# Hybrid decoder block on 8 cores: the constants on VectorE are prepared behind the third conv channel tile instead of ahead of the first scalings of x

## The reference

```python
h = concat([meta, x])                                # (B, 16 + 2048, 1024)
u = rms_norm(h, norm_mix_g) @ w_in                   # 2576 columns
c_val, c_gate, q, k, v, g, gate_lr = split(u)
# conv group, 512 channels
y = depthwise_causal_conv(c_val * sigmoid(c_gate), conv_w, width=31) + conv_b
y_conv = silu(layer_norm(y) * conv_ln_g + conv_ln_b)
# gated linear attention, 4 heads, chunks of 64
log_a = log_sigmoid(gate_lr @ w_gate2 + gate_b) / 16
y_gla = rms_norm(chunked_attention(q, k, v, log_a), gla_norm_g) * silu(g)
h = h + concat([y_conv, y_gla]) @ w_out
h = h + (silu(n @ w_ffn_gate) * (n @ w_ffn_up)) @ w_ffn_down     # n = rms_norm(h, norm_ffn_g)
return rms_norm(h, norm_final_g)[:, 16:]
```

## Time and profile before

| | |
|---|---|
| median of 3 runs | 1551.28 us |
| time of the profiled execution | 1555.21 us |
| its span on the slowest core (core 4) | 1553.7 us |
| spans of the 8 cores | 1530.8 to 1553.7 us |
| TensorE busy | 1444.6 us, 93% |
| VectorE, ScalarE, GpSimd busy | 790.7, 546.5, 266.8 us |
| DMA | 297.55 MB moved, mean 192 GB/s |
| mean granted TensorE clock, cores | 0.983 to 0.989 |

### The profile page before, as it was taken

How to read it: one execution, slowest core, us unless ns; L and a number is a source line. 1 busy time by engine, 2 the same in 40 slices (tenths; PEclk the granted TensorE clock), 3 DMA queues, 4 the chain that set the end, 5 groups by cost and what they waited for, 6 DMA issues and landing times.

```text
span 1553.7 us, 26365 instructions; the slowest of 8 cores (1530.8 to 1553.7 us)
## 1 busy us (share of the span) xinstructions
PE 1444.6 (93%) x8290; PEld 690.4 (44%) x8290; DVE 790.7 (51%) x1739; ACT 546.5 (35%) x964; POOL 266.8 (17%) x359
## 2 busy tenths in 40 slices
PE   0878799999999999999999999999999999999995
PEld 0444454444444444444444444444444445444442
DVE  2368448525565246544384445744475454744324
ACT  2465362415424254224433054222542245211101
POOL 2042151122510123001400024001320023000000
PEclk9989899999999999999999999999999999999998
DMA  9568898899978984499745986379744975365551
GB/s 185 130 165 206 189 199 172 180 233 270 252 203 208 253 272 129 137 201 250 231 136 159 215 247 197 126 199 249 232 141 144 219 243 181 123 197 175 198 163 55
DMA packets 127992, 297.55 MB, mean 192 GB/s; under 512 B 48992, under 2 KB 59616, under 8 KB 127856
## 3 DMA queue, kind: packets, MB, share of 16 engines
q1 hardware_dynamic: 65424, 199.92, 40.6%
q0 software_dynamic: 23904, 86.49, 25.3%
q10 hardware_dynamic: 38528, 9.44, 4.7%
HBM read 276.22 MB, written 46.40 MB: 208 GB/s over the span
## 4 chain that ended last, share of the span: by engine, by line
PE 81%; DMA 11%; issue 3%; ACT 2%; DVE 2%; POOL 0%; SPq 0%; DVEq 0%; ACTq 0%; POOLq 0%
PE ps L671 58%; PE ps L1288 18%; DMA wring<-wsc 4%; DMA wring<-wpack 4%; DMA small<-gla_norm_g 2%; PE ps L650 1%; PE ps L758 1%; DMA h<-xin 1%; DMA out<-h 1%; PE ps L868 0%; PE ps L1191 0%; PE ps L1164 0%; PE ps L1159 0%; ACT rep L1023 0%; DVE xn_tm L637 0%
## 5 line engine op out<-in xcount | busy, mean ns | idle before, releaser
L671 PE MATMUL ps<-x2T,wring 128*128 128x512 bf16 (+1 forms) x2912 | 641.7, 375 | 18.5 <-DMA wring<-wsc 9.6
L671 PEld LDWEIGHTS ps<-x2T,wring 128*128 128x128 bf16 x2912 | 278.2, 98 | 343.4 <-issue 37.6
L1288 PE MATMUL ps<-wring,actT 128*128 128x512 bf16 x1408 | 310.8, 379 | 1.2 <-DMA wring<-wpack 1.2
L1272 DVE SCALAR_TENSOR_TENSOR ftmp<-ftmp,ps 128x512 f32<-128x512 f32 x176 | 120.7, 686 | 253.7 <-ACT ftmp L1271 245.1
L1271 ACT ACTIVATE ftmp<-ps 128x512 f32<-128x512 f32 x176 | 105.2, 598 | 349.4 <-PE ps L671 328.2
L1288 PEld LDWEIGHTS ps<-wring,actT 128*128 128x128 bf16 x1408 | 136.5, 98 | 168.8 <-issue 8.8
L671 PE MATMUL ps<-xT,wring 128*128 128x512 bf16 x736 | 168.4, 385 | 4.7 <-ACT xT L655 2.0
L1274 DVE SCALAR_TENSOR_TENSOR actT<-ftmp,ps 128x512 bf16<-128x512 f32 x176 | 120.1, 686 | 45.1 <-PE ps L671 41.3
L671 PE MATMUL ps<-wring,xT 128*128 128x512 bf16 x512 | 120.6, 385 | 5.4 <-DMA wring<-wpack 3.4
L671 PE MATMUL ps<-wring,yT 128*128 128x512 bf16 x512 | 119.9, 383 | 6.0 <-issue 3.7
L671 PEld LDWEIGHTS ps<-xT,wring 128*128 128x128 bf16 x736 | 71.9, 99 | 92.0 <-issue 10.7
(11 more groups left out here) (179 smaller groups left out, 1220.6 us busy)
## 6 DMA issues: line engine op xcount, KB each, us to landing
wring<-wsc SPq DMA_DIRECT2D x303, 512.0 KB, 5.1
wring<-wpack POOLq DMA_DIRECT2D x75, 512.0 KB, 9.6
wsc<-wring SPq DMA_DIRECT2D x48, 512.0 KB, 6.8
h<-xin POOLq DMA_DIRECT2D x28, 512.0 KB, 12.6
out<-h POOLq DMA_DIRECT2D x28, 512.0 KB, 5.4
rep<-vsc POOLq DMA_DIRECT2D x24, 543.0 KB, 7.9
rep<-vsc SPq DMA_DIRECT2D x8, 543.0 KB, 6.4
yT<-rep SPq DMA_DIRECT2D x64, 64.0 KB, 3.5
```

The lines of the kernel that those rows point to most:

```text
L671: ins = e.matmul(pt_ap, lhsT=lhs(kc), rhs=rhs(kc), start=(kc == 0), stop=(kc == KC - 1))
L1272: P.add("dve", lambda e: e.scalar_tensor_tensor(out=th[:], in0=th[:], scalar=1.0, in1=pg[:], op0=ALU.add, op1=ALU.mult), R=[Bpg, Bth], W=[ ...
L1288: ins = e.matmul(ps[t][:], lhsT=actT[:, j, t * 128:(t + 1) * 128], rhs=wd3[:, j - j0, :], start=(j == 0), stop=(j == NJ - 1))
```

## The change

The four instructions become a function, `build_consts`, which the unit "wcv" calls first. Their rank is now that of "wcv", and the first of them also reads `BvT[2]`, the buffer of the third conv channel tile's values: it waits until VectorE has written them. The loads of the constants, their order and their semaphore stay. In the changed kernel line numbers are higher by 1 to 3 from here on (637 is 639, 792 is 794).

```diff
@@ -556,15 +556,17 @@
                         R=[Bpar, Bact[9]], W=[Bpar])
             Bpar = Buf("par")
 
-            allc = list(cbufs)
-            P.add("dve", lambda e: e.tensor_scalar(out=gb[:], in0=gb[:], scalar1=-1.0, scalar2=None, op0=ALU.mult),
-                  R=allc, W=[Bc])
-            P.add("dve", lambda e: e.tensor_scalar(out=cvec[:, 1:3, :], in0=cvec[:, 1:3, :], scalar1=0.5, scalar2=None,
-                                                   op0=ALU.mult), R=[Bc], W=[Bc])
-            P.add("dve", lambda e: e.tensor_scalar(out=gng[:], in0=gng[:], scalar1=0.5, scalar2=None, op0=ALU.mult),
-                  R=[Bc], W=[Bc])
-            P.add("dve", lambda e: e.tensor_scalar(out=convw4[:], in0=convw4[:], scalar1=0.5, scalar2=None, op0=ALU.mult),
-                  R=[Bc], W=[Bc])
+            def build_consts():
+                allc = list(cbufs)
+                P.add("dve", lambda e: e.tensor_scalar(out=gb[:], in0=gb[:], scalar1=-1.0, scalar2=None, op0=ALU.mult),
+                      R=allc + [BvT[2]], W=[Bc])
+                P.add("dve", lambda e: e.tensor_scalar(out=cvec[:, 1:3, :], in0=cvec[:, 1:3, :], scalar1=0.5, scalar2=None,
+                                                       op0=ALU.mult), R=[Bc], W=[Bc])
+                P.add("dve", lambda e: e.tensor_scalar(out=gng[:], in0=gng[:], scalar1=0.5, scalar2=None, op0=ALU.mult),
+                      R=[Bc], W=[Bc])
+                P.add("dve", lambda e: e.tensor_scalar(out=convw4[:], in0=convw4[:], scalar1=0.5, scalar2=None, op0=ALU.mult),
+                      R=[Bc], W=[Bc])
+
             Bwcv = [Buf(f"wcv{c}") for c in range(4)]
 
             def build_wcv():
@@ -820,6 +822,7 @@
                 if meta:
                     @unit(0.1, "wcv")
                     def _():
+                        build_consts()
                         build_par()
                         build_wcv()
```

## The result

The changed kernel takes 1537.37 us (median of 20 runs), the kernel before 1553.33 (median of 20). The ratio is 0.9897, 95% interval 0.988 to 0.9915: 16.0 us less (13.2 to 18.6), which by the bound of 2% counts as the same. Comparisons here leave out executions in which one die ran disturbed, so a median over all of them can lie elsewhere than a ratio says. The profiled execution took 1536.04 us; its slowest core is core 1 with a span of 1534.5 us, and the spans go from 1514.6 to 1534.5.

The account below looks back on a forecast made before the run. TensorE, busy 1444.6 of 1553.7 us, bounds the kernel; an edit pays only where it stands still. The terms -18.5 + 0.7 - 0.9 = -18.7 us, from the median 1551.28, gave 1532.6 us, range 1525 to 1540.

Parts of the forecast that it names:

- The start, -18.5: On core 4, VectorE's first scaling of x no longer waits for the constants' loads: 34.15 to 15.65, 18.5 us earlier.
- One of the prediction's own signs against itself: At the start, the prediction counts as wrong if the first scaling waits for `gmix` or an x tile; no size.
- The work behind moves with the shift.: Behind the first scaling, no load at a fixed time swallows the gain, so the 18.5 us count in full.
- The new place of the constants, +0.7: Moved instructions around the third and fourth tiles' values delay TensorE's gate product and the scan: +0.7 us, ends 0 and +1.5.
- The first scratch write, about 10 us: Issued at about 37 beside weight loads, it takes about 10 us, landing at 47 before the copies' issue at 50.
- The copies and the x tiles, -0.9: Before the second block, ScalarE's 4.56 us wait for the fourth x tile is traded for one in front: net -0.9 us.
- rival 1: Shift partly spent at scratch and copies: ScalarE's squares precede the decays, k and q wait; 1537.4 to 1540.5 us, chance 0.16.
- rival 1's milder form: Only the +3.9 us from late second-block x tiles comes: -13.9 us, 1537.4 us; within a chance of 0.16.
- Rival 3: The start is bound by the loads, with the DMA engines full: gain near zero, 1549 to 1553 us, chance 0.03.
- rival 4: Copies back are caught behind weight loads and land 22.1 us late: slower, 1554.9 us, chance 0.02.
- rival 5: Something else ahead of the scalings in VectorE's list waits for the same semaphore, so the change fails; chance below 0.01.
- Rival 2: More than the shift: the fourth tile's 4.56 us wait is won whole, 1526.6 to 1528.2 us, chance 0.13.

Follow-up runs that it names:

- VectorE's list alone: Kernel before with only the twelve constant and product instructions moved in VectorE's order to where the changed kernel has them, other engines' lists unchanged: ratio 0.989, -15.4 us mean of cores.
- third set: Runs on one chip with the changed kernel measured a third time, unaltered, against the kernel before: ratio 0.9861, -18.4 us in the mean of cores.

## Why the prediction was right, and where a size was off

The forecast was 1532.6 us and its range 1525 to 1540; the median is 1537.37. Of the difference of 4.8 us, 2.1 lie in the kernel before (1551.28 in three runs, 1553.33 in twenty) and 2.7 in the sum (-18.7 against -16.0). The three comparisons of the changed kernel give -16.0, -13.2 and -21.6 us on the slowest core; the second and third give -16.0 and -18.4 in the mean of cores. So the sum is as good as the measurement can tell, within about 3 us. One of its small terms was met in size by something else, which is luck, and another is not shown at all, as told below.

- **The start, -18.5.** Measured over the cores -17.9, -18.2 and -17.6. The mechanism is shown: VectorE's list alone does it, an earlier last load does most of it, and a later one costs 6.4 us before and nothing after. On core 4 the first scaling came at 17.2 and not at 15.65, because its 1/sqrt steps began 1.5 us later than in the profile before; on core 1 it moved by 19.9 (20.1 was expected), on core 6 by 18.4 (16.2). The wait of a core was a poor measure of its own shift: what a core's x tiles take from one execution to the next goes into both. One of the prediction's own signs against itself showed: the first scaling waits for `gmix`, 1.08 us on core 0 and 2.50 on core 7 (0.2 us on one core and 0.3 to 1.2 on three in the two later profiles). The gain's load is the next bound at the start, and on single cores it is already reached; the forecast had only core 4's, which lands 0.85 us before it is wanted.
- **"The work behind moves with the shift."** Right. Behind the first scaling no load holds it up: the conv moves 17.3 to 17.6 us, and TensorE waits for no weight tile between 23 and 50 on any core. What the forecast didn't have is TensorE's pace at the start. Its first eight projection matmuls take about 3.5 us and later groups of eight 1.89, though the granted clock reads 1.00 all the while. The second eight were still slow on two cores before (4 and 6) and are on five in the changed kernel (24.01 and 28.42 on core 1, above). On these five the shift shrinks by 1.8 to 2.5 us from the first scaling to the gate, on cores 4 and 6, which now have it fast, it grows by 2.1 to 2.2, and on core 7, fast in both, it changes by 0.3. That is the 0.7 us that the mean loses there (-17.9 to -17.2). In the third set's profile three cores are slow, and 0.1 us is lost.
- **The new place of the constants, +0.7.** Too much. The gate product waited 0.24 us instead of up to 0.7, and from the low-rank gate to the conv the shift doesn't change (-17.2, -17.3; in the third set -17.5, -17.6). The term was 0.24 at most: the two ends that I had, 0 and 1.5, held it, and it lay at the lower one. That 0.7 us are missing all the same at the conv is luck: they are TensorE's slower pace, which another execution needn't have, and not the constants.
- **The first scratch write, about 10 us.** It took 10.0 on core 1 (issued at 38.02) and landed at 48.0, before the copies were issued at 50.6. The rule of the Trainium skill ("DMA: Bandwidth & Descriptors", section "Queues, rings and completion order"), from which I had worked out twice the 1.9 us, was too short by 6 us here: the measurement decides. It changed nothing in the sum, as forecast.
- **The copies and the x tiles, -0.9.** The first copy took 6.3 us and the second 9.1 on core 1, where I had used 6.8 for both, so the conv had 3.5 us to spare and not 5. The wait for the fourth x tile is gone and ScalarE waits for the first, as forecast. What I hadn't named in the sum is TensorE behind it, 0.7 to 1.7 us for `k_in` on seven cores (4.0 on one core of the third set's profile). That is rival 1's chain in small. It is paid back at the next places: TensorE's waits for `q_in` (0.9 to 3.9 us on four cores before) are gone, and the one at line 1046 (now 1049) falls from 2.3 to 3.9 us to 1.7 to 1.8 on every core. Net, from the conv to `x2T`: +0.6, -0.8 and +0.4 us in three executions; the -0.9 can't be told from zero.
- **Rivals.** The median, 1537.4, is the very number of rival 1's milder form, but not its course: by it the shift would have fallen to 13.9 us behind the conv, and at the second block's conv it is 16.3 to 17.7. Rival 3 (bound by the loads) falls with the shift at the conv, rival 4 with the copies that landed by 60.4 on core 1, rival 5 with the missing wait. Rival 2 would have needed the fourth tile's wait won whole; it was traded.

## What to carry to other kernels

An engine's list is strict: look at the head of it for an instruction that isn't on the way to the first matmul but waits for a late load, even one of 0.2 us on half a kilobyte. Put it behind the first work that has all it needs, and far enough that its load has landed: one step behind the scalings left 2.1 of 17.5 us at the conv, behind the third channel tile all of it was kept. This scheduler, whose model has the load landed in time, needed a dependency to keep it there; a lower rank did nothing. Then look at what is late next: here the gain's load, on two cores of eight.

## What the runs showed of the hardware

- The same load of 0.5 KB took 23.2 to 27.1 us over the cores as the last of its queue beside the weight tiles (25.19 on core 4), 3.3 to 4.2 at the head of the queue, and 27.7 to 32.9 with one more 512 KB load ahead of it.
- A scratch write of 136 KB that takes 1.9 us beside an idle queue took 10.0 to 11.5 us over the cores while the last weight tiles were on their way.
- One stop of TensorE cost a little more than its length. In the version with the constants behind the scalings TensorE stood 12.4 us in the mean. From the first projection to the conv the cores needed 53.7 us and in the changed kernel 39.0; of these 14.7 us, 12.6 are idle time and 2.2 are matmuls that ran slower. On core 2 the granted clock fell to half of full speed (1.2 GHz) at 33.0, during the stop (29.2 to 41.9), and rose at 50.1. Up to 135 us the records have half speed for 28.6 us in the mean of cores, against 11.6 to 14.5 in three profiles of the changed kernel and 12.4 in that of before. The window from 30 to 50 us on core 2, first in that version and then in the changed kernel:

```profile
30.00:50.00 20.00, 6.81 (x39) 4.36 (x40) 9.24 (x22) 1.30 (x2) 0.00 (x0) 0.58 0.70 117
```

```profile
30.00:50.00 20.00, 17.75 (x143) 10.10 (x141) 8.02 (x22) 4.99 (x12) 0.29 (x1) 1.00 0.87 155
```

- The recorded clock doesn't tell every slow stretch. Core 6 of that version has a granted clock of 1.00 from 30 to 55 us. Yet behind its stop of 11.07 us eight matmuls of 512 columns take 3.29 us, and only later 1.89, as elsewhere at full speed:

```profile
48.23 3.29 PE L673 MATMUL ps<-xT,wring 128*128 128x512 bf16 x8
...
53.03 1.89 PE L673 MATMUL ps<-xT,wring 128*128 128x512 bf16 x8
```

- Two neighbouring cores can sit at a granted clock of 0.81 for some 150 us (cores 2 and 3 from 108.5 and 108.3 us, in one profile) while the other cores of their die don't. How often a pair does so depended on the order of the work (8 and 6 of 13 executions, against 4 of 83 of the other kernels on the same two chips).
